# Two-block transformer kernel: order of the output projections, first expert pair's weight loads, last tiles of the final norm

## The reference, cut to what matters

```python
for i in range(2):
    sh1, sc1, g1, sh2, sc2, g2 = split(silu(c) @ ada_w[i] + ada_b[i])
    h = rms_norm(x, norm1_g[i]) * (1 + sc1) + sh1
    # i = 0: differential attention; i = 1: stick-breaking attention, 16 heads
    x = x + g1 * (attention(h) @ w_out)            # output projection, 1024 x 1024
    h = rms_norm(x, norm2_g[i]) * (1 + sc2) + sh2
    # router: top group of 4, then top 2 of its 8 experts; 32 experts,
    # hid = silu(xb @ w_gate[e]) * (xb @ w_up[e]);  y = hid @ w_down[e]
    x = x + g2 * hierarchical_moe(h)
return rms_norm(x, final_norm_g)
```

## Time and profile before

| | before |
|---|---|
| median of 3 runs | 2512.28 us (2511.5 to 2519.03) |
| profiled execution | 2513.37 us |
| its span | 2511.3 us |
| TensorE products, busy | 2256.0 us (90%) |
| TensorE weight loads, busy | 1023.5 us (41%) |
| VectorE, busy | 611.6 us (24%) |
| ScalarE, busy | 436.2 us (17%) |
| POOL, busy | 263.7 us (10%) |
| weights' DMA queue (q1) | 548.72 MB, 54.6% of 16 engines' span |

### The profile page before, as it was taken

One profiled execution on the slowest core, in us unless ns is written; L12 is line 12 of the kernel. 1 busy time (PEld: TensorE's weight loads), 2 busy tenths in 40 slices (PEclk: granted clock), 3 DMA queues, 4 the chain that ended last, 5 costly groups with the idle time before them and its releaser, 6 DMA issues. The chain is left out here.

```text
span 2511.3 us, 22477 instructions
## 1 busy us (share of the span) xinstructions
PE 2256.0 (90%) x8750; PEld 1023.5 (41%) x8750; DVE 611.6 (24%) x1328; ACT 436.2 (17%) x814; POOL 263.7 (10%) x508
## 2 busy tenths in 40 slices
PE   8999999999999998898878777899899888888776
PEld 4454454444444444473322222344454733322222
DVE  2364522111003007441111010320373411111113
ACT  2222311000003005311000000110373111000001
POOL 3122111000000001211111111000121111111110
PEclk9999999999999999999999999999999999999998
DMA  7468825211312103057999999930003589999995
GB/s 260 176 217 291 328 80 202 75 42 67 112 67 101 67 0 135 17 219 329 418 427 428 428 425 410 385 117 8 34 1 134 215 345 423 428 428 426 425 421 235
DMA packets 128023, 586.78 MB, mean 234 GB/s; under 512 B 17896, under 2 KB 29552, under 8 KB 103372
## 3 DMA queue, kind: packets, MB, share of 16 engines
q1 hardware_dynamic: 112480, 548.72, 54.6%
q0 software_dynamic: 14864, 36.76, 3.9%
q10 hardware_dynamic: 604, 0.27, 0.0%
HBM read 571.31 MB, written 30.65 MB: 240 GB/s over the span
## 5 line engine op out<-in xcount | busy, mean ns | idle before, releaser
L221 PE MATMUL ps<-hT,ring 128*128 128x512 f32 (+3 forms) x1328 | 561.3, 585 | 4.2 <-issue 4.2
L1903 PE MATMUL ps<-ring,arena 128*64 128x512 f32 x1920 | 448.7, 607 | 91.8 <-ACT arena L1949 51.9
L221 PEld LDWEIGHTS ps<-hT,ring 128*128 128x128 f32 (+1 forms) x1328 | 249.4, 190 | 313.5 <-issue 309.8
L1938 PE MATMUL ps<-ring,arena 128*64 128x512 f32 x960 | 247.7, 675 | 54.7 <-DMA ring<-in_expert_w_down 45.3
L1903 PEld LDWEIGHTS ps<-ring,arena 128*64 128x64 f32 x1920 | 141.8, 139 | 368.4 <-issue 285.5
L228 PE MATMUL ps<-ring,hT 128*128 128x512 f32 x512 | 225.4, 599 | 0.8 <-ACT hT L1543 0.7
L1938 PEld LDWEIGHTS ps<-ring,arena 128*64 128x64 f32 x960 | 84.7, 154 | 197.0 <-issue 186.2
L228 PEld LDWEIGHTS ps<-ring,hT 128*128 128x128 f32 x512 | 97.4, 192 | 120.4 <-issue 118.8
L1978 DVE TENSOR_TENSOR arena<-ps,arena 128x512 f32<-128x512 f32 x32 | 22.1, 691 | 509.8 <-PE ps L1903 509.8
L1065 PE MATMUL ps<-ring,arena 128*128 128x512 f32 x336 | 144.8, 592 | 0.8 <-issue 0.8
L1983 DVE TENSOR_TENSOR arena<-ps,arena 128x1024 f32<-128x1024 f32 x30 | 36.7, 1224 | 323.6 <-PE ps L1938 323.6
(11 more groups left out here) (370 smaller groups left out, 2186.0 us busy)
## 6 DMA issues: line engine op xcount, KB each, us to landing
ring<-in_expert_w_gate SPq DMA_DIRECT2D x60, 2048.0 KB, 16.1
ring<-in_expert_w_down SPq DMA_DIRECT2D x60, 2048.0 KB, 17.1
ring<-in_expert_w_up SPq DMA_DIRECT2D x60, 2048.0 KB, 17.9
ring<-in_ada_w SPq DMA_DIRECT2D x24, 2048.0 KB, 11.6
ring<-in_diff_w_in SPq DMA_DIRECT2D x6, 2048.0 KB, 8.1
ring<-in_sb_w_in SPq DMA_DIRECT2D x6, 2048.0 KB, 19.7
ring<-in_ffn_w_gate SPq DMA_DIRECT2D x5, 2048.0 KB, 14.0
ring<-in_ffn_w_val SPq DMA_DIRECT2D x5, 2048.0 KB, 13.8
```

The costliest lines, as they stand in the source:

```text
L221: mm = pe.matmul(out, w[:, c, cols], x[:, c, :], start=(c == 0), stop=(c == chunks - 1))
L1903: mm = pe.matmul(k.ps[slots, 2 + kind, :], k.xT[:, c, slots], w[:, c, :], start=(c == 0), stop=(c == KD - 1))
L1938: mm = pe.matmul(k.ps[slots, 5 + half, :], k.hTt[:, c, slots], w[:, c, half * 512:(half + 1) * 512], start=(c == 0), stop=(c == KH - 1))
```

## The change

It has four parts.

1. `sb_tensor` begins tiles 0 and 1 of the output projection too: parts 0 and 1 ahead of the last sums, parts 2 to 7 ahead of the last values, parts 8 to 31 behind them. A part is one product (one chunk, one tile, one half). The first part waits until VectorE has read all scores (`a.scores_read`).
2. In `out_proj_tensor` with `begun`, in both layers, the turns and logits stand one tile later: tile 2, turn 0, tile 3, turn 1, logits 0, then turn 2, logits 1, the filler products, turn 3, logits 2 and 3.
3. Pair 1's second up piece and first down piece are loaded by halves; the first halves wait for a new semaphore that TensorE raises when half of pair 0's gate products are done.
4. At the end, tile 2 of the last layer is placed `whole` as tile 3 is, its two additions leave VectorE, and the norms of tiles are interleaved with the additions of the tile after next. In the first layer no tile is `whole`.

Beside these, POOL's `m.turn` semaphore is replaced by an existing one.

```diff
@@ squares and norms
-def rstd_vector(dve, s, tt):
+def var_vector(dve, s, tt):
 
     col = slice(tt, tt + 1)
     s.after(dve, "sq", tt + 1)
     dve.tensor_scalar(s.vr[:, col], s.ss[:, col], 1.0 / D, EPS, ALU.mult, ALU.add).then_inc(s.sems["var"], 1)
+
+
+def root_vector(dve, s, tt):
+
+    col = slice(tt, tt + 1)
     s.after(dve, "root", tt + 1)
     dve.reciprocal(s.rstd[:, col], s.rt[:, col]).then_inc(s.sems["rstd_set"], 1)
     s.after(dve, "rstd_set", tt + 1)
+
+
+def rstd_vector(dve, s, tt):
+    var_vector(dve, s, tt)
+    root_vector(dve, s, tt)
...
+def gained_vector(dve, k, s, tt, gain):
     dve.scalar_tensor_tensor(out=k.x[:, tt, :], in0=k.x[:, tt, :], scalar=s.rstd[:, tt:tt + 1], in1=gain,
@@ out_proj_parts
         if n == 0:
-            pe.wait_ge(a.biased, 2 * DIFF_UNITS)
+            pe.wait_ge(*a.scores_read)
@@ out_proj_tensor
-        if tt:
-            turn_tensor(pe, k, m.norm, tt - 1)
-        if tt >= 2:
-            logits_tensor(pe, k, m, tt - 2)
+        if tt > begun // 2:
+            turn_tensor(pe, k, m.norm, tt - 1 - begun // 2)
+        if tt - begun // 2 >= 2:
+            logits_tensor(pe, k, m, tt - 2 - begun // 2)
+    if begun:
+        turn_tensor(pe, k, m.norm, TT - 2)
+        logits_tensor(pe, k, m, TT - 3)
@@ sb_tensor
+        if p == SB_PAIRS:
+            out_proj_parts(pe, k, a, range(0, 2))
         if 1 <= p <= SB_PAIRS:
             sums(p - 1)
+        if p == SB_PAIRS + 1:
+            out_proj_parts(pe, k, a, range(2, 8))
         if p >= 2:
             values(p - 2)
-    pe.wait_ge(a.oT_out, SB_PAIRS)
+    out_proj_parts(pe, k, a, range(8, 4 * KD))
@@ moe_sync
+    def half_weights(source, dst, expert, chunks, half, landed):
+        n = SLOT_F // 2
+        src = source[expert, :, :].rearrange("(p k) n -> p k n", k=chunks)[:, half * chunks // 2:(half + 1) * chunks // 2, :]
+        sp.dma_start(dst[:, half * n:(half + 1) * n].rearrange("p (k n) -> p k n", k=chunks // 2), src).then_inc(landed, 16)
     up(1, 0, m.up1_landed)
-    sp.wait_ge(m.gated, 2)
-    up(1, 1, m.up1_landed)
-    down(1, 0, m.down1_landed)
+    places = moe_places(k, 1)
+    for half in range(2):
+        if half:
+            sp.wait_ge(m.gated, 2)
+        else:
+            sp.wait_ge(m.half_gated, 1)
+        half_weights(m.w_up, places[1][1], 3, KD, half, m.up1_landed)
+        half_weights(m.w_down, places[2][0], 2, KH, half, m.down1_landed)
     sp.wait_ge(m.upped, 2)
@@ moe_tensor, hidden
+                if first and kind == 0 and c == KD // 2 - 1:
+                    mm.then_inc(m.half_gated, 1)
@@ last_slots_vector
-    for c in range(2):
-        weight = k.weights[:, c * TT + TT - 1:c * TT + TT]
+    for n, tt in enumerate(whole):
+        for c in range(2):
+            weight = k.weights[:, c * TT + tt:c * TT + tt + 1]
...
@@ placed_tensor
+    whole = tt in t.whole
@@ tail_semaphores
+    t.whole = (TT - 2, TT - 1) if l else ()
@@ second_part, tensor
-            out_proj_tensor(pe, k, a, m)
+            out_proj_tensor(pe, k, a, m, begun=2)
@@ second_part, vector, the end
+            placed_vector(dve, k, last, 0)
+            placed_vector(dve, k, last, 1)
             for tt in range(TT):
-                placed_vector(dve, k, last, tt)
-                if tt == 0:
-                    combine_vector(dve, k, t, last, 2)
-                row_norm_vector(dve, k, final, tt, k.gain_2)
+                var_vector(dve, final, tt)
+                if tt + 2 < TT:
+                    placed_vector(dve, k, last, tt + 2)
+                root_vector(dve, final, tt)
+                gained_vector(dve, k, final, tt, k.gain_2)
```

More of the change, by code:

```diff
@@ L210, in row_norm_vector @@
     rstd_vector(dve, s, tt)
+    gained_vector(dve, k, s, tt, gain)
+def gained_vector(dve, k, s, tt, gain):
     dve.scalar_tensor_tensor(out=k.x[:, tt, :], in0=k.x[:, tt, :], scalar=s.rstd[:, tt:tt + 1], in1=gain,
@@ L1887, in moe_tensor, with hidden @@
     halves = (slice(0, BLOCK), slice(BLOCK, P))
-    def hidden(i, pair, gate_landed, up_landed):
+    def hidden(i, pair, gate_landed, up_landed, first=False):
         places = moe_places(k, pair)
@@ L1924, in moe_tensor @@
         count = 32 * (pair // 2) + 32
-        hidden(pair, pair, (gate_landed, count), (up_landed, count))
-        results(pair, (down_landed, count))
+        more = 16 * (pair % 2)
+        hidden(pair, pair, (gate_landed, count), (up_landed, count + more), first=(pair == 0))
+        results(pair, (down_landed, count + more))
     last = last_pair(pe, k, m)
@@ L1930, in moe_tensor @@
         results(0, (m.down_landed, i * 32 + 96))
-    hidden(last, 0, (m.gate1_landed, 96), (m.up1_landed, 96))
+    hidden(last, 0, (m.gate1_landed, 96), (m.up1_landed, 112))
 def down_half(pe, k, downs, half):
@@ L1995, in moe_vector, with last_slots_vector @@
     hidden(last)
-    last_slots_vector(dve, k, m, ch, last)
-def last_slots_vector(dve, k, m, ch, last):
+    last_slots_vector(dve, k, m, ch, last, t.whole)
+def last_slots_vector(dve, k, m, ch, last, whole):
     ch.mark(dve.tensor_copy(k.last_weight, k.slot_weight[:, bass.ds(last, 1)]))
@@ L2008, in last_slots_vector @@
                                          ALU.is_equal, ALU.mult))
-    for c in range(2):
-        weight = k.weights[:, c * TT + TT - 1:c * TT + TT]
-        done = ch.mark(dve.tensor_scalar(k.last_diag[:, c, :], k.ident[:, :], weight, None, ALU.mult))
+    for n, tt in enumerate(whole):
+        for c in range(2):
+            weight = k.weights[:, c * TT + tt:c * TT + tt + 1]
+            done = ch.mark(dve.tensor_scalar(k.last_diag[:, 2 * n + c, :], k.ident[:, :], weight, None, ALU.mult))
     ch.after(done)
@@ L2020, in last_results_tensor, with placed_tensor @@
     pe.wait_ge(cb.ys_set, 2)
-def placed_tensor(pe, k, t, cb, tt, whole=False):
+def placed_tensor(pe, k, t, cb, tt):
+    whole = tt in t.whole
     if whole:
@@ L2031, in placed_tensor @@
         for c in range(2 * whole):
-            mm = pe.matmul(out, k.last_diag[:, c, :], k.yg[:, 2 * tt + c, cols], start=False, stop=(c == 1))
+            mm = pe.matmul(out, k.last_diag[:, 2 * t.whole.index(tt) + c, :], k.yg[:, 2 * tt + c, cols], start=False, stop=(c == 1))
     mm.then_inc(cb.placed, 1)
@@ L2105, in moe_rows_gpsimd @@
         pool.wait_ge(m.xg_clear, i * 2 + 3)
-        pool.sem_inc(m.turn, 1)
+        pool.sem_inc(m.table_ready, 1)
         gather(k.index_x)
@@ L2528, in layer_semaphores @@
      m.x_turned, m.xT_act, m.xT_dve, m.gate_landed, m.up_landed, m.down_landed, m.gated, m.upped, m.downed, m.hidden,
-     m.silu, m.h_turned, m.hT_out, m.y_dve, m.xg_clear, m.y_indexed, m.turn, m.table_ready, m.hot, m.tabled, m.indexed,
-     m.gate1_landed, m.up1_landed, m.down1_landed) = semaphores(
+     m.silu, m.h_turned, m.hT_out, m.y_dve, m.xg_clear, m.y_indexed, m.table_ready, m.hot, m.tabled, m.indexed,
+     m.gate1_landed, m.up1_landed, m.down1_landed, m.half_gated) = semaphores(
         nc, f"moe{l}_", """router_landed logits diffs exps chosen ranked routed rows_stored x_landed x_turned xT_act
         xT_dve gate_landed up_landed down_landed gated upped downed hidden silu h_turned hT_out y_dve
-        xg_clear y_indexed turn table_ready hot tabled indexed
-        gate1_landed up1_landed down1_landed""")
+        xg_clear y_indexed table_ready hot tabled indexed
+        gate1_landed up1_landed down1_landed half_gated""")
     m.w_gate, m.w_up, m.w_down = (w[n][l] for n in ("expert_w_gate", "expert_w_up", "expert_w_down"))
@@ L2803, in _ @@
             for tt in range(TT):
-                placed_tensor(pe, k, k.tails[1], last, tt, whole=(tt == TT - 1))
+                placed_tensor(pe, k, k.tails[1], last, tt)
         @block.vector
```

3 lines of the change are left out of this document (2 added, 1 removed).

## The result

The changed kernel takes 2493.31 us (median of 4 runs, 2486.8 to 2495.88) against 2511.89 us before (4 runs, 2509.67 to 2519.03): a ratio of 0.9921, with an interval of 0.9907 to 0.9935. That is 18.6 us less. I had forecast 11.3, with bounds of 6 and 17 for the forecast's own case, and the gain lies above them. The direction was right; the sum was too small, and the later parts look for the missing 7.3 us. The profiled execution of after took 2495.88 us, its span is 2494.0 us.

The account below looks back on a forecast made before the run. TensorE sets the time up to pair 3's gates, then the weights' stream, so pair 0's shift brings the end forward equally. Terms 6.6 + 4.9 + 0 - 0.2 = 11.3 us gave 2501 us, range 2493 to 2508.

Parts of the forecast that it names:

- the forecast's own case: Whole kernel: the four parts gain their forecast terms, time between 2495 and 2506 us; chance 0.60.
- the gather taken at 4.5: Second layer, ahead of pair 0: the gather, held for the final norm's row, comes 4.5 us earlier.
- the clock at 0.4: Second layer, pair 0: a shorter TensorE stand ahead of it improves the granted clock, worth 0.4 us of 0 to 2.9.
- First layer (6.6 forecast): First layer's output projection: tile 2 ahead of the first turn covers tile 0's norm; last turn and pair 0 6.6 us earlier.
- Second layer, TensorE (2.9): Second layer, last scores to last turn: projection parts among the pairs fill TensorE's stands, 2.9 us.
- My own terms, 5.2 less 0.88 and 1.36: Behind tile 3: it ends 5.2 us earlier, but VectorE first waits for turn 1 (0.88) and empties it (1.36).
- Gates by halves (0): Pair 1's half loads, both layers: the stream runs 4 us ahead, then stands 4 us longer for pair 3; gain 0.
- Rival A: Both layers' first later loads: a queue, not TensorE, stops the stream, so halves gain 4 us a layer: 2493; chance 0.13.
- The end (-0.2): After the last down: interleaving hides ScalarE's square, but TensorE's extra 3.4 us replaces it; 0.2 us slower.
- B: Second layer: its shift is lost at the final norm's row or pair 0's clock, 1 us or less remaining: 2505; chance 0.15.
- C: Expert stages: the bandwidth plateau bounds from before pair 3 on, and the shifts are given back there: 2511; chance 0.08.
- Rival D: Pair 1's half loads: shorter rows run slower; 5.8 us lost a layer at half rate, 2532 at a third; chance 0.04.

Follow-up runs that it names:

- the second layer's part with the two moves: Kernel before plus the second layer's projection among pairs and new order, final norm's row loaded early, GpSimd's addition delayed behind the gather: 2501.14 us, ratio 0.9958.

## Why the prediction fell short

In short: the terms for TensorE and the halves held, and what failed is the second layer's term behind TensorE's 2.9 us, the gather taken at 4.5 and the clock at 0.4. The layer was forecast at 4.9 us; alone it was timed at 8.5 and is 6.5 by its stretches.

**First layer (6.6 forecast).** Right. From the end of the last part to the filler it was 40.0 us (1061.72 to 1101.73 in the trace) and is 33.4 (1058.37 to 1091.81): 6.6. The stand of 0.34 us ahead of the last turn is gone too, which makes 7.1 at the turn. The part alone was timed at 7.3. The other 1.5 us of the layer's stretches (0.5 of it between filler and gather) lie ahead of the edit or behind the filler, and two profiles of one kernel differ there as much.

**Second layer, TensorE (2.9).** Right in size, 2.80, and the order was needed for it, which the prediction used only for "turn 1 and logits 0 (2.6 us) now stand behind tile 3" and never priced in this layer: the old order would have cost 7.2.

**Second layer, the gather ("I take 4.5").** This step failed: the term was too small, and the weighing behind it was wrong. I weighed two causes for the landing of the final norm's row, GpSimd's issue (3.2 us earlier) and the weights' drain (5.2 earlier), and took a value between. Measured against the values, the weights' issue moved 5.46 us (1967.78 to 1956.30, less the 6.02 by which the values had moved), the row's issue 3.30, and the gather 5.63. The landing went with the weights to 0.2 us; the row's own issue did not matter. Ten profiles with the late row show it, old order and new: the row lands 33.3 to 33.6 us behind the weights' issue in all of them, but 24.4 to 24.6 us behind its own issue in six and 22.1 to 22.5 in four. By the rule of the Trainium skill (DMA: Bandwidth & Descriptors, Queues, rings and completion order), as I read it, the landing would follow its own issue, which gives 3.2 us; no trace here agrees with that reading. (My own terms, 5.2 less 0.88 and 1.36, give 3.0 for that issue.) What the runs show in its place: the row lands when the weights on the way have drained, also those issued after it. In before, bandwidth falls to 205 and 18 GB/s in the windows of 2 us at 1998 and 2000, and the row lands at 2001.22. So the full 5.2 was to be taken. The clock was the other small term: I took 0.4 us, and gather to `later` gave 0.9. With that the layer gave 6.5 by its stretches, not 4.9.

**Gates by halves (0).** Taken out of after they are worth nothing, by the mechanism given; put into before they gave 2.3 us by the ratio, inside the noise, so 0 to 3 is what the runs allow. The longer stand came in the first layer only. Rival A, which would have given 2493, the time measured, falls: the time came out there for other reasons.

**The end (-0.2).** The stands came where they were put, for tiles 2 and 3; the sum was 0.7 us too high, and the part gives 0.46 us, which the times can't show. But after's own profile has 3.0 us less: its last downs take 7.09 us where before has 8.78, both for the same products (granted clock 0.63 and 0.51 in before's windows of 2 us at 2476 and 2478, 1.00 throughout in after), and begin 0.8 us sooner after their load's issue. In the second profile of after they take 8.78 again. So the last pair's downs vary between executions of one kernel, and the part does not decide it. Fast downs alone don't make the end short either: two other profiles (before with halves, and the second layer's part with the two moves) have 7.09 us, begin them 1.7 us later, and end as late as the rest.

**The sum.** Of the missing 7.3 us, 1.5 are in the first layer's stretches, 1.6 in the second's, 1.9 at the end (0.7 the part, the rest the last pair of one profile), and 2.3 in stretches that no edit touches. The single parts were timed at 7.3, 8.5, 0 to 3 and 0 to 1, so 16 to 20 with 18.6 measured: they add up. What the traces can lay to an edit is less, 7.1, 6.5 and 0.5, in sum some 14 us; the 4.5 us beyond it are laid to no part (1.3 of them are the last pair's). As to the rivals, the second layer's shift reached pair 0, against B, and nothing was given back on the plateaus, against C. Rival D had half loads slowing the stream: with them the stream runs ahead. The plateaus' own gains (0.8 and 1.3 us) lie within what they vary by over all 14 profiles (358 to 361 us, and 353 to 357).

**What stays open.** Where the 4.5 us go that the stretches don't hold. Why kernels that differ only in later code reach the first load up to 3 us apart (954.1 to 957.4), and what decides the clock of the last pair. Why GpSimd's addition stopped VectorE's step in the second layer and not in the first. For the 8.5 us timed and the 6.5 us counted of the second layer's part I have no further place; the interval of the times (5.3 to 11.8) holds both.

## What to carry to other kernels

Work begun early, chunk by chunk over two tiles, finishes both together, and what used to hide behind the second tile stands bare: move the order with it, or the stand only changes its place (2515 against 2502.6 us here). Before timing a wait by the engine's queue, find what drains with it: a small load issued behind large ones landed with the last of them, so it belongs far ahead of them. And when a stand is taken away, look at what now runs side by side; a 2.4 us addition on GpSimd cost 5.9 us from values to `later` (200.0 against 194.1), more than the 2.5 us by which the gather came earlier.

## What the runs showed of the hardware

- A step of VectorE on 128x4 elements, 0.16 us alone, took 3.19 us beside a GpSimd addition over 128x1024 elements, and 0.16 again when that ran 1.4 us behind the gather. In the first layer of the same profile, 0.05 us nearer to the gather's start, it took 0.16 us with the addition in its old place.
- A stand of 2.34 us ahead of pair 0 was followed by a granted clock of 0.50 and gates and ups of 16.43 us; with a stand of 1.24 us, and with none, the clock stayed at 1.00 and they took 13.95. Taking away the last two microseconds of a stand was worth more than they are: 5.1 us from values to `later` (199.2 to 194.1).
- A transfer of one row, broadcast to 128 partitions, took 22.1 to 24.6 us from its issue when weights were on the way, and landed 33.3 to 33.6 us behind the first of these weights' issues in ten profiles. Issued early it took 3.7 to 3.9 us in three kernels and 11.2 in a fourth.
